# Gated DeltaNet samples: keys and decayed queries in one product per state

## The reference

```python
decay = jnp.where(incl, jnp.exp(jnp.where(incl, diff, 0.0)), 0.0)
M = jnp.eye(C, dtype=F32) + jnp.where(strict, beta[..., :, None] * kk * decay, 0.0)
u = lax.linalg.triangular_solve(M, v * beta[..., None], left_side=True, lower=True)
w = lax.linalg.triangular_solve(M, k * (beta * jnp.exp(G))[..., None], left_side=True, lower=True)
Aqk = jnp.einsum('nbhtk,nbhsk->nbhts', q, k) * decay
qg = q * jnp.exp(G)[..., None]
...
v_new = uc - jnp.einsum('bhtk,bhkv->bhtv', wc, S)
o = jnp.einsum('bhtk,bhkv->bhtv', qc, S) + jnp.einsum('bhts,bhsv->bhtv', ac, v_new)
S = glc[..., None, None] * S + jnp.einsum('bhsk,bhsv->bhkv', kc, v_new)
```

## Time and profile before

| | |
|---|---|
| median of 3 runs | 1950.11 us |
| the profiled execution | 1954.44 us, span 1952.6 us |
| PE matmul, weight load busy | 94%, 89% of the span |
| DVE, ACT, POOL busy | 58%, 28%, 26% |
| mean granted TensorE clock | 0.945 |

### The profile page before, as it was taken

How to read it: one execution, slowest core, us unless ns; L and a number is a source line. 1 busy time by engine, 2 the same in 40 slices (tenths; PEclk the granted TensorE clock), 3 DMA queues, 4 the chain that set the end, 5 groups by cost and what they waited for, 6 DMA issues and landing times.

```text
span 1952.6 us, 34456 instructions
## 1 busy us (share of the span) xinstructions
PE 1825.9 (94%) x13505; PEld 1746.2 (89%) x13505; DVE 1123.1 (58%) x1845; ACT 540.3 (28%) x992; POOL 503.9 (26%) x285
## 2 busy tenths in 40 slices
PE   7999999999999999996899999999998899999996
PEld 7888888898999999996889888888887899999996
DVE  5777777765716161676567666766643553535353
ACT  4444444433100000113244434434422200000011
POOL 3000000001565656561000000000000355555562
PEclk8998989899999999998899999999789899999997
DMA  6122222232232322231220221122012123232321
GB/s 198 55 66 58 66 62 66 66 88 68 87 87 87 87 86 86 86 77 33 57 64 17 56 68 32 42 60 67 12 57 66 46 87 91 87 90 86 87 75 46
DMA packets 257853, 136.79 MB, mean 70 GB/s; under 512 B 6747, under 2 KB 256053, under 8 KB 257781
## 3 DMA queue, kind: packets, MB, share of 16 engines
q1 hardware_dynamic: 219920, 115.01, 20.7%
q10 hardware_dynamic: 37860, 20.76, 3.7%
HBM read 123.75 MB, written 12.00 MB: 70 GB/s over the span
## 4 chain that ended last, share of the span: by engine, by line
PE 46%; DVE 4%; ACT 2%; issue 1%; ACTq 0%; DVEq 0%
PE pj L497 30%; PE rr L793 2%; PE rr L786 2%; PE rr L757 2%; PE rr L518 1%; PE rr L535 1%; PE rr L775 1%; PE rr L692 1%; PE rr L702 1%; PE rr L767 1%; DVE ol L1991 1%; PE rr L862 1%; DVE pr L1757 0%; PE rr L712 0%; PE rr L867 0%
## 5 line engine op out<-in xcount | busy, mean ns | idle before, releaser
L458 POOL TENSOR_SCALAR w_hi<-w_raw 128x1024 fp32r<-128x1024 f32 x137 | 145.8, 1064 | 1402.4 <-PE pj L497 1374.0
L497 PE MATMUL pj<-xh,w_hi 128*128 128x272 f32 x2064 | 466.0, 308 | 9.0 <-DVE w_lo L1536 6.2
L497 PE MATMUL pj<-xh,w_lo 128*128 128x272 f32 x2064 | 441.7, 297 | 0.0
L497 PE MATMUL pj<-xl,w_hi 128*128 128x272 f32 x2064 | 439.6, 295 | 0.0
L497 PEld LDWEIGHTS pj<-xh,w_hi 128*128 128x128 f32 x2064 | 335.3, 195 | 30.5 <-issue 19.7
L460 POOL TENSOR_TENSOR w_lo<-w_raw,w_hi 128x1024 fp32r<-128x1024 f32 x137 | 354.6, 2588 | 11.4
L497 PEld LDWEIGHTS pj<-xl,w_hi 128*128 128x128 f32 x2064 | 337.3, 196 | 0.0
L497 PEld LDWEIGHTS pj<-xh,w_lo 128*128 128x128 f32 x2064 | 337.1, 197 | 0.0
L497 PE MATMUL pj<-oh,w_hi 128*128 128x272 f32 x1248 | 264.6, 293 | 5.9 <-DVE w_lo L1536 3.1
L497 PE MATMUL pj<-oh,w_lo 128*128 128x272 f32 x1248 | 259.6, 290 | 0.0
L497 PE MATMUL pj<-ol,w_hi 128*128 128x272 f32 x1248 | 259.2, 289 | 0.0
(11 more groups left out here) (307 smaller groups left out, 2318.1 us busy)
## 6 DMA issues: line engine op xcount, KB each, us to landing
w_raw<-in_mlp_w_up_dram SPq DMA_DIRECT2D x64, 512.0 KB, 4.0
w_raw<-in_mlp_w_down_dram SPq DMA_DIRECT2D x64, 512.0 KB, 4.0
w_raw<-in_hgrn_w_in_dram SPq DMA_DIRECT2D x32, 512.0 KB, 4.1
w_raw<-in_gdn_w_in_dram SPq DMA_DIRECT2D x32, 512.0 KB, 4.1
out_dram<-S ACTq DMA_DIRECT2D x16, 512.0 KB, 3.3
w_raw<-in_hgrn_w_out_dram SPq DMA_DIRECT2D x9, 512.0 KB, 3.8
w_raw<-in_gdn_w_out_dram SPq DMA_DIRECT2D x9, 512.0 KB, 4.0
S<-in_state_hgrn_dram ACTq DMA_DIRECT2D x8, 512.0 KB, 4.1
```

The costliest lines, as they stand in the source:

```text
L458: nc.gpsimd.tensor_scalar(w_hi[:, s], w_raw[:, j], 1.0, 1.0, ALU.mult, ALU.mult).then_inc(hi_pool, 1)
L497: last = mm(pj[:, s, b, 0:HALF], w[:, s, k, :], v[:, k, b * HALF:(b + 1) * HALF], start=(k == 0 and a == 0), stop=(k == end - 1 and a == 2))
```

## The change

At level 8, PE multiplies each state once, with eight columns: the sample's four keys and its four decayed queries (`K` and `qe` are neighbouring rows of `ws`, now read together as `kq`). The result is held in bank 1 as (sample, keys or queries, token), `of_state`. DVE forms `sr1` from the key half and then copies the query half to a spare row (`oss`), and PE waits for `oss` where it waited for `sr1`. At level 64 only the product of `vns` with A is left; DVE adds the spare row to it (`os`), ahead of `pred64`, in place of ACT's copy. What waited for ACT's `os` (the product `w`) or PE's (the decay of the samples' states) now waits for DVE's, or for nothing; `vbig`, whose place the spare row shares, waits for it too.

```diff
+        kq = ws[:, 8:10]
+        oss = gd["spare"][:, 0:TS]
...
+        of_state = rr[:, 1, 0:2 * TS].rearrange("p (b a n) -> p b a n", b=NSEQ, a=2)
...
                     if m == 8:
                         pe.wait_ge(v.sem, v.after("tt4", h))
                         pe.wait_ge(st_in, h * 16 + 16 * (H + 1))
+                        pe.wait_ge(va.sem, va.after("qe", h))
                         for b in range(NSEQ):
-                            last = mm(rr[:, 1, b * SLEN:(b + 1) * SLEN], S0[:, b, :],
-                                      K[:, TP + b * SLEN:TP + (b + 1) * SLEN], start=True, stop=True)
+                            last = mm(of_state[:, b], S0[:, b, :], kq[:, :, TP + b * SLEN:TP + (b + 1) * SLEN],
+                                      start=True, stop=True)
                         t.did(last, "sks")
                     if m == 64:
                         pe.wait_ge(s.sem, s.after("vns", h))
                         pe.wait_ge(v.sem, v.after("tt32", h))
-                        mm(rr[:, 1, 0:TS], oo[0:TS, VNS:VNS + P], A[0:TS, TP:T], start=True, stop=False)
-                        for b in range(NSEQ):
-                            last = mm(rr[:, 1, b * SLEN:(b + 1) * SLEN], S0[:, b, :],
-                                      qe[:, TP + b * SLEN:TP + (b + 1) * SLEN], start=False, stop=(b == NSEQ - 1))
-                        t.did(last, "os")
+                        t.did(mm(rr[:, 1, 0:TS], oo[0:TS, VNS:VNS + P], A[0:TS, TP:T], start=True, stop=True), "os")
...
                     if m == 8:
-                        pe.wait_ge(v.sem, v.after("sr1", h))
+                        pe.wait_ge(v.sem, v.after("oss", h))
...
-                        pe.wait_ge(s.sem, s.after("os", h))
+                        pe.wait_ge(v.sem, v.after("os", h))
...
-                    if m == 64:
-                        sem_of(t, "os", h)
-                        s.did(f(oo[:, TP:T], rr[:, 1, 0:TS], ACT.Copy), "os")
...
-                        v.did(tt(rt[:], rr[:, 1, 0:TS], eGs[:, NC:], ALU.mult), "sr1")
+                        v.did(tt(blocks(rt[:], SLEN), of_state[:, :, 0], blocks(eGs[:, NC:], SLEN), ALU.mult), "sr1")
+                        v.did(cp(blocks(oss[:], SLEN), of_state[:, :, 1]), "oss")
...
+                    if m == LEVELS[-1]:
+                        after(t, "os", h)
+                        after(v, "oss", h)
+                        v.did(tt(gd["oo"][:, TP:T], rr[:, 1, 0:TS], oss[:], ALU.add), "os")
...
                 after(s, "vns", h)
+                after(v, "os", h)
                 v.did(apart(gd_vbig, gd["oo"][0:TS, VNS:VNS + P]), "vbig")
...
-                        after(t, "os", h)
                         v.did(decay_samples(eGs[:, NC:]), "sdec")
```

More of the change, by code:

```diff
@@ L250, in build @@
                 "qe", "cols2", "nbe"],
-            gr=["pred2", "tt2", "vb", "pred4", "tt4", "kdt", "kbt", "kdts", "gate", "sr1", "pred8", "tt8", "sr2", "sr3", "pred16", "tt16",
-                "pred32", "tt32", "pred64",
+            gr=["pred2", "tt2", "vb", "pred4", "tt4", "kdt", "kbt", "kdts", "gate", "sr1", "oss", "pred8", "tt8", "sr2", "sr3", "pred16", "tt16",
+                "pred32", "tt32", "os", "pred64",
                 "vbig", "S0", "sdec", "S1", "S2", "S3", "sn0", "sn1"],
@@ L269, in build @@
                 "K", "tm0", "zsig"],
-            gr=["x2", "x4", "x8", "x16", "x32", "rs", "vns", "x64", "os",
+            gr=["x2", "x4", "x8", "x16", "x32", "rs", "vns", "x64",
                 "vn0", "w", "vn1", "vn2", "vn3", "oo", "sq"],
```

## The result

The changed kernel takes 1966.76 us in the median (1959.54 to 1968.03), the kernel before beside it 1949.19: the ratio over their runs is 1.0073, with a 95% interval of 1.0051 to 1.0095 (the two medians alone would give 1.0090). A later comparison gave 1.0042 (1.0023 to 1.0061). By these ratios it is slower by some 8 to 14 us; 1959 had been forecast. The ratios leave out runs that count as slow, more than 1.5% above the fastest of their kernel; that concerns one of the twelve runs with the products back (1966.63 us) and four of the twelve of the dense fill (1968.3 to 1976.4 us), whose mean with all its runs is 0.2% above that of the kernel before.

What follows compares the result with a forecast made beforehand. The chain of waits lay on PE nearly everywhere, with DVE's list to `pred64` meeting it. Terms: -1.7 (products) + 1.1 (copy) + 1.1 (sum) + 8.6 (clock) = +9.1 us on 1950.1, so 1959 us, range 1945 to 1969.

Steps and rivals of the forecast that it cites:

- Gain on PE hidden behind `pred64`: Level 64: removing the products gains only PE's lateness against `pred64`, 0.27 us a head in heads 0 to 5.
- Head 7: Last head: PE's second tile needs low parts from DVE, so removing the products gains only 0.1 us.
- Copy and sum: DVE's `oss` behind `sr1` and `os` ahead of `pred64`: 0.15 us each, 1.1 us each over heads 0 to 6.
- Wider product at no cost: Level 8: eight columns instead of four cost between 0 and 0.1 us a head, taken as 0.
- The clock: Behind `pred64`: idle PE brings a lower granted clock on the dense work, +8.6 us; this forecast case had chance 0.50.
- 1.72, the price of each drop that the loop does show: Behind `pred64`: 1.72 us of full-speed work lost per drop, charged in five of the heads 0 to 5.
- Gain hidden, clock as before: Behind `pred64`: PE idles 3.2 us, the work behind runs at full clock; about 1950.5 us, chance 0.25.
- The gain arrives: Level 64: `pred64` doesn't hold PE, 12 us are won; 1938 us, chance 0.10.
- Long drops: Behind `pred64`: lower clock lasts as behind 1512, 3.45 us in each of six heads; 1971 us, chance 0.15.

Runs made afterwards that it cites:

- products back: Changed kernel with the eight level-64 products put back on PE as dead work, every added step kept: 1948.19 us, ratio 0.9972 to the kernel before.
- dense fill: Changed kernel with six dead 272-column products between `dt64` and `kk` of heads 0 to 6: 1952.14 us, ratio 0.9971 to the kernel before.
- 64 columns: Changed kernel with each state multiplied by 64 columns instead of eight at level 8: 1967.34 us, ratio 1.0062 to the kernel before.
- the kernel before with the earlier sum: Kernel before with low parts moved ahead of the key norm and queries behind `pred64` on DVE: 1953.81 us, ratio 1.0009.
- level-8 fill alone: Changed kernel with three dead 272-column products at level 8 ahead of the wait for `oss`: 1966.48 us, ratio 1.0054 to the kernel before.
- the earlier sum and 64 columns: Changed kernel with 64 columns per state, low parts ahead of the key norm and queries behind `pred64` on DVE: 1950.49 us, ratio 0.9982.
- sum earlier: Changed kernel with low parts moved ahead of the key norm and queries behind `pred64` on DVE: 1947.84 us, ratio 0.9977 to the kernel before.

## Why the prediction was right, and what was mis-sized

*Gain on PE hidden behind `pred64`: right in heads 0 to 6.* The removed products ended up as the 3.24 us of idle time that the prediction put at 3.2, and `pred64` ends 6.95 us behind the start of the key norm (1272.74 - 1265.79; 7.0 was named). The rest of the gain was put too high: PE takes up the tile 0.23 us behind `pred64` (1272.97 - 1272.74), not 0.05, which I had read at `sr1`. Against 0.32 before that is 0.09 a head instead of 0.27.

*Head 7: a wrong reading that hardly shows in the sum.* The prediction held the gain there to 0.1 by the low parts of L1536. But PE runs through its tiles without waiting for them, and `pred64` had waited for PE all along. The rows are `pred64` of head 7 before and after, then 4 us from the tile behind PE's next longer wait (2.03 us in both), again before and after:

```profile
1481.95 0.42 DVE L1902 COPY ws<-rr 64x256 f32<-64x256 f32 x1 [5.67 <-PE rr L831]
1486.05 0.42 DVE L1905 COPY ws<-rr 64x256 f32<-64x256 f32 x1 [3.77 <-PE rr L832]
...
1492.00:1496.00 4.00, 4.00 (x32) 4.00 (x33) 0.00 (x0) 1.23 (x2) 0.00 (x0) 1.00 0.49 134
1496.00:1500.00 4.00, 3.93 (x23) 3.96 (x24) 0.00 (x0) 0.28 (x2) 0.00 (x0) 0.70 0.46 131
```

`pred64` starts 7.22 instead of 9.01 us behind the end of `vns`, 1.79 earlier, so the products' time is won in full; a drop that the kernel before doesn't have there then takes some 1.5 us of it back. The 0.1 came out nearly right by luck.

*Copy and sum: right in place, priced half too high.* Each is 0.18 us long, but the instruction behind it starts 0.10 later (L1900 at 1272.23, L1905 at 1272.33), so 0.10 a step and 1.4 us in all, not 2.2. With 6 x 0.09 = 0.5 won in heads 0 to 5 and 1.8 - 1.5 = 0.3 in head 7, +0.6 stands for the forecast +0.5, by errors that cancel.

*Wider product at no cost: right.* 256 ns a pass against 253, and the sixteen of a head take 1.90 us as before; with 64 columns it is 275 and 1.95. L712, named in the prediction as a row for 64 columns, has 128 a pass.

*The clock: right mechanism, its price too low. This is the mis-sized term.* The prediction charged one drop of 1.72 us in five heads, 8.6 us. The head of before takes 68.25 us in heads 1 to 4; the changed one 71.62, 71.61, 70.92, 71.21, so +2.7 to +3.4. Take 0.2 for copy and sum off, give back the 0.09, and the clock costs 2.6 to 3.3 a head. The term that was too small is "1.72, the price of each drop that the loop does show": in heads 3 and 4 the low clock around `pred64` is longer than the drops of before (3.1 us of work in head 4), and in heads 1 and 2 a second one is no longer free at level 8 (1.66). The prediction saw that both drops of before were hidden, and then asked only for one of them what a moved head does to it. That the stretch between first and last `pred64` still grew by just 8.6 us is in part chance: heads 1 to 4 alone are 12.4 us longer, but the profiled run of before had a 71.21 us head 5 (69.71 after), and the stretch holds the 1.8 us won in head 7.

*Rivals.* "Gain hidden, clock as before" falls by the rows at 0.50. "The gain arrives" falls by the 3.24 us wait, in all heads but the last. "Long drops" named 3.45 a head: some heads come near it, by another route than the one long drop that it described.

The Trainium skill, "TensorE: Matmul & The Clock Gate", section "HAM oscillation — how this bites in real kernels", says of a matmul loop waiting for DMA that the wait throttles the work behind it in every turn of the loop. The dense fill agrees, for a wait for VectorE: 3.24 us of waiting filled, and 0.50 became 1.00 behind it.

*Open.* What sets a head at 68.3 or at 71.6 us, whatever is moved by a microsecond inside it, I could not settle: before and five of the kernels made from the change sit at 68.3, the changed kernel and the one with 64 columns at 71.6. The change alone doesn't decide it, for the kernel before with the earlier sum had heads of 71.5 as well in its profiled run, the longest of twelve (1972.13 us), while its median is that of the kernel before. Nor is it settled why the level-8 fill alone gives its gain back, or what brings the drop at level 8. That one isn't idle PE: in the kernel before PE is busy without a break ahead of it, 1.90 us of it with state products, and the clock falls at 1239 all the same:

```profile
1237.09 1.90 PE L767 MATMUL rr<-ws,S 128*128 128x4 f32 x16
...
1236.00:1239.00 3.00, 3.00 (x29) 2.99 (x28) 2.42 (x7) 0.12 (x1) 0.00 (x0) 1.00 0.00 0
```

## What to carry to other kernels

Before removing PE work, look for what PE meets next: if that is a wait, the time becomes idle time, and the granted clock of the stretch behind the wait decides whether the edit is neutral or slower. Bring the awaited engine forward as well, or keep PE busy through the wait, and then recheck each drop that used to be hidden, since a head that moves against its drops exposes others. Compare such kernels by many interleaved runs, as one profile can hold a head or two with a drop more; and say which of the runs was profiled.

## What the runs showed of the hardware that was not expected

- More TensorE work took less time: six dead products a head (3.02 us of PE) took the ratio from 1.0073 or 1.0042 to 0.9971, with a wide scatter. With the earlier sum and 64 columns, two at one wait took it from 0.9982 to 0.9966 (the intervals overlap), and three more at the other to 0.9916.
- A pass that loads a 128 x 128 f32 state has a record of 253 ns with 4 columns, 256 with 8 and 275 with 64; the drop at level 8 stayed with all three.
- PE started 0.06 us behind the end of `oss` (1106.49 to 1106.55, a wait of 1.61 us) and 0.23 us behind that of `pred64` (a wait of 3.24 us). What makes the difference isn't shown.
- The lower clock behind a wait came with 3.05 to 3.25 us of idle PE ahead of the tile (changed kernel), and not with 1.2 to 1.4 us there (sum earlier, heads 0 to 5). A stretch of 3.00 us with PE busy all along, 1.90 of it products that load states for four columns, was followed by the lower clock too.
